# Retention by head pairs, head statistics in 32-row array tiles, splits ahead of row parts in the mixing stage

## What is computed

```python
xn = rms_norm_2(h, norm_mix_g[layer])
sb_q, sb_k, sb_v, r_q, r_k, r_v, r_g = jnp.split(xn @ w_in[layer], split_at, axis=-1)
y_sb = from_heads(stick_breaking_attention(sb_q, sb_k, sb_v)) @ w_sb_out[layer]
rq, rk = rotary(r_q), rotary(r_k) * RET_QK_DIM ** -0.5
y_ret = retention_chunkwise(rq, rk, rv)      # 8 heads, scores * decay table, times v
y_ret = y_ret * lax.rsqrt(jnp.mean(y_ret * y_ret, axis=-1, keepdims=True) + EPS)
y_ret = from_heads(y_ret) * ret_norm_g[layer]
y_ret = (jax.nn.silu(r_g) * y_ret) @ w_ret_out[layer]
g_sb, g_ret = jnp.split(jax.nn.sigmoid(xn @ w_gate[layer] + b_gate[layer]), 2, axis=-1)
h = h + (g_sb * y_sb + g_ret * y_ret) @ w_out[layer]
```

## Time and profile before

| | us |
|---|---|
| median of 3 runs | 1920.4 |
| lowest and highest | 1918.1, 1921.41 |
| profiled execution, its own time | 1920.54 |
| span of its trace | 1918.8 |
| PE / DVE / ACT busy | 1850.8 / 1354.7 / 950.0 |

### The profile page before, as it was taken

How to read it: one execution, slowest core, us unless ns; L and a number is a source line. 1 busy time by engine, 2 the same in 40 slices (tenths; PEclk the granted TensorE clock), 3 DMA queues, 4 the chain that set the end, 5 groups by cost and what they waited for, 6 DMA issues and landing times.

```text
span 1918.8 us, 31594 instructions
## 1 busy us (share of the span) xinstructions
PE 1850.8 (96%) x12127; PEld 1615.2 (84%) x12127; DVE 1354.7 (71%) x1976; ACT 950.0 (50%) x1481; POOL 0.2 (0%) x4
## 2 busy tenths in 40 slices
PE   4999999999999999999999999999999979999997
PEld 3777777776977899999999999999988967777786
DVE  5789999986777776677666666676866653347797
ACT  3325665753345454455345544455445443336685
POOL 0000000000000000000000000000000000000000
PEclk8999999999999999999999999999999989999999
DMA  9757987986411366666666465665545346779894
GB/s 327 230 174 243 297 273 228 299 249 188 127 34 45 110 186 184 179 192 182 181 185 177 115 196 172 179 181 168 155 130 156 119 162 224 273 263 350 308 352 197
DMA packets 516492, 383.11 MB, mean 200 GB/s; under 512 B 13825, under 2 KB 474122, under 8 KB 516242
## 3 DMA queue, kind: packets, MB, share of 16 engines
q1 hardware_dynamic: 515856, 381.15, 64.0%
q10 hardware_dynamic: 514, 0.30, 0.1%
HBM read 380.35 MB, written 1.05 MB: 199 GB/s over the span
## 4 chain that ended last, share of the span: by engine, by line
PE 89%; DVE 5%; ACT 2%; SPq 1%; DMA 1%; issue 1%; DVEq 0%; ACTq 0%
PE ps L2460 18%; PE ps L2462 18%; PE ps L2461 18%; PE ps L3146 3%; PE ps L3148 3%; PE ps L3147 3%; PE ps L2473 2%; PE ps L2474 2%; PE ps L2475 2%; PE ps L3176 2%; PE ps L3174 2%; PE ps L3175 2%; PE ps L3162 1%; ACT hi L1003 1%; DVE lo L1527 1%
## 5 line engine op out<-in xcount | busy, mean ns | idle before, releaser
L2460 PE MATMUL ps<-nhi,hi 128*128 128x258 f32 (+2 forms) x1920 | 589.7, 307 | 0.0
L2462 PE MATMUL ps<-nhi,lo 128*128 128x258 f32 (+2 forms) x1920 | 588.0, 306 | 0.0
L2461 PE MATMUL ps<-nlo,hi 128*128 128x258 f32 (+2 forms) x1920 | 586.0, 305 | 0.0
L1527 DVE TENSOR_TENSOR lo<-raw,hi 128x1024 fp32r<-128x1024 f32 (+2 forms) x388 | 460.4, 1188 | 113.9 <-ACT hi L1003 113.0
L1003 ACT ACTIVATE hi<-raw 128x1024 fp32r<-128x1024 f32 (+2 forms) x388 | 395.7, 1024 | 236.8 <-PE ps L2462 178.1
L2460 PEld LDWEIGHTS ps<-nhi,hi 128*128 128x128 f32 x1920 | 364.5, 190 | 27.4 <-issue 9.1
L2462 PEld LDWEIGHTS ps<-nhi,lo 128*128 128x128 f32 x1920 | 363.7, 189 | 16.9
L2461 PEld LDWEIGHTS ps<-nlo,hi 128*128 128x128 f32 x1920 | 363.6, 189 | 16.4
L2460 PE MATMUL ps<-hhi,hi 128*128 128x256 f32 (+1 forms) x576 | 177.2, 308 | 0.0
L2461 PE MATMUL ps<-hlo,hi 128*128 128x256 f32 (+1 forms) x576 | 176.6, 307 | 0.0
L2462 PE MATMUL ps<-hhi,lo 128*128 128x256 f32 (+1 forms) x576 | 176.6, 307 | 0.0
(11 more groups left out here) (431 smaller groups left out, 2984.0 us busy)
## 6 DMA issues: line engine op xcount, KB each, us to landing
raw<-in_ffn_w_gu SPq DMA_DIRECT2D x176, 512.0 KB, 4.6
modw<-in_w_mod SPq DMA_DIRECT2D x56, 1024.0 KB, 7.3
raw<-in_ffn_w_d SPq DMA_DIRECT2D x64, 512.0 KB, 4.3
raw<-in_w_in SPq DMA_DIRECT2D x36, 512.0 KB, 4.0
raw<-in_w_exp_gate SPq DMA_DIRECT2D x36, 512.0 KB, 5.4
raw_more<-in_w_exp_up SPq DMA_DIRECT2D x36, 512.0 KB, 5.4
mod_early<-in_w_mod SPq DMA_DIRECT2D x16, 1024.0 KB, 10.3
raw<-in_w_exp_down SPq DMA_DIRECT2D x32, 512.0 KB, 6.6
```

Source lines behind the costliest of these rows:

```text
L1527: v.tensor_tensor(lo[:, s], raw[:, s], hi[:, s].bitcast(F32), ALU.subtract).then_inc(lo_ready, 1)
L2460: pe.matmul(bank(u, T), w_hi(u, k), h_, start=(k == 0), stop=False)
L2461: pe.matmul(bank(u, T), w_hi(u, k), l_, start=False, stop=False)
L2462: ins = pe.matmul(bank(u, T), w_lo(u, k), h_, start=False, stop=(k == nk - 1))
```

## The change

Six edits:

- In `sbq` and `sbk`, ACT's `rows_hi` runs one slab later, behind the split of the next slab; the first scores `Z_AT[0]` go from T = 0 to T = 1 and DVE's part `SOFT_AT[0]` from 1 to 2.
- Retention goes by pairs of heads: at T = 34, 36, 38, 40 the scores of two heads, one on rows 0 to 63 and one on rows 64 to 127 of the array, into banks 4 and 5; one decay product of 768 columns; at T = 35, 37, 39, 41 v for both heads; one copy of 512 columns; one square of 512 columns, all into a buffer `ret_sq` of their own.
- Decay tables come for two heads at a time, in two buffers: 4 loads instead of 8.
- Sums of squares of all eight heads at T = 43, in one go, head h into the 32-column tile h % 4 of the array; the attention norm's `o_sum` likewise. Statistics then occupy 128 partitions. Spreads take 32 rows each: four heads at T = 45, four at T = 47.
- The sigmoid of the gates goes from T = 36..43 to T = 32..39. The root goes ahead of `rg`'s first SiLU on ACT.
- Scaling at T = 45..48, gating and splits head by head from T = 45 on; six heads beside `rg` instead of five.

The core of the diff:

```diff
-Z_AT = (0, 9, 17, 26)
-SOFT_AT = (1, 10, 19, 27)
+Z_AT = (1, 9, 17, 26)
+SOFT_AT = (2, 10, 19, 27)
-GATE_AT = 36
+GATE_AT = 32
-ROOT_AT = 45
-SPREAD_AT = 47
-RET_FULL = {48: (0, 1), 49: (2, 3), 50: (4, 5), 51: (6, 7)}
-RET_HI = {49: (0, 1), 50: (2, 3), 51: (4,)}
-RET_BESIDE = 5
+RET_SUM_AT = 43
+ROOT_AT = 43
+SPREAD_AT = (45, 47)
+RET_SCALE = {45: (0, 1), 46: (2, 3), 47: (4, 5), 48: (6, 7)}
+RET_GATE_AT = 45
+RET_BESIDE = 6
...
+        def tile_of(h):
+            return slice(TILE * (h % TILES), TILE * (h % TILES + 1))
+        def tile_sums(h):
+            return const("head_sums")[:, TILE * (h // TILES):TILE * (h // TILES + 1)]
+        def tile_rows(h):
+            return head_rows[tile_of(h), P * (h // TILES):P * (h // TILES + 1)]
+        def pair_decay(p):
+            return decay[:, 2 * (p % 2) * DEC_W:2 * (p % 2 + 1) * DEC_W]
...
-            plain("sbq", side=rows_hi)
-            plain("sbk", side=lambda c: rows_hi(U + c))
+            plain("sbq", side=lambda c: rows_hi(c - 1) if c else None)
+            plain("sbk", side=lambda c: rows_hi(U + c - 1))
+            rows_hi(KD - 1)
...
                 b = T - GATE_AT
                 if 0 <= b < KD:
-                    act.wait_ge(evacuated, U * ph["sbout"][0])
+                    act.wait_ge(evacuated, U * ph["gates"][0] + 2 * b + 2)
...
+                for p in range(HEAD_PAIRS):
+                    if T == RET_AT + 2 * p + 1:
+                        dve.wait_ge(S["ro_done"], p + 1)
+                        v.tensor_copy(yr[:, 2 * p * SEQ:2 * (p + 1) * SEQ], bank(6 + p % 2)).then_inc(S["ro_full"], 1)
+                    if T == RET_AT + 2 * p:
+                        dve.wait_ge(S["rs_done"], p + 1)
+                        dve.wait_ge(S[f"in_dec{p % 2}"], 16 * (p // 2 + 1))
+                        if p >= 2:
+                            dve.wait_ge(S["ro_done"], p - 1)
+                        v.scalar_tensor_tensor(out=wk3(p % 2), in0=two(4), scalar=0.125, in1=pair_decay(p).rearrange("p (a n) -> p a n", a=2),
+                                               op0=ALU.mult, op1=ALU.mult).then_inc(S["rw_done"], 1)
...
+            def ret_gate(h):
+
+                y = yr[:, h * SEQ:(h + 1) * SEQ]
+                dve.wait_ge(S["ro_scaled"], h + 1)
                 dve.wait_ge(evacuated, U * ph["rg"][0] + h + 1)
                 v.tensor_tensor(y, y, rg[:, h * SEQ:(h + 1) * SEQ], ALU.mult).then_inc(S["mix_full"], 1)
...
+                        pe.wait_ge(S["rw_done"], p + 1)
...
+                        for j in range(2):
+                            h, w = 2 * p + j, wk3(p % 2)[:, j]
+                            pe.matmul(bank(6 + p % 2, SEQ, j * SEQ), rvt[:, h * P:(h + 1) * P], w[:, 0:SEQ], start=True, stop=False)
+                            ins = pe.matmul(bank(6 + p % 2, P, j * SEQ + P), rvt[:, D + h * P:D + (h + 1) * P], w[:, SEQ:DEC_W], start=False, stop=True)
+                        ins.then_inc(S["ro_done"], 1)
...
+                        for j in range(2):
+                            ins = pair_scores(4 + j, rk, rq, j, p)
+                        ins.then_inc(S["rs_done"], 1)
+                if T == RET_SUM_AT:
+                    pe.wait_ge(S["ro_sq"], HEAD_PAIRS)
+                    for h in range(HEADS):
+                        ins = pe.matmul(bank(6, SEQ, parts=tile_of(h)), tile_sums(h), ret_sq[:, h * SEQ:(h + 1) * SEQ], start=(h < TILES), stop=(h >= TILES))
+                    ins.then_inc(S["ro_ss"], 1)
+                for b in range(HEAD_BATCHES):
+                    if T == SPREAD_AT[b]:
+                        if b == 0:
+                            pe.wait_ge(S["ro_rstd"], 1)
+                        else:
+                            pe.wait_ge(S["ro_scaled"], b * TILES)
+                        for h in range(b * TILES, (b + 1) * TILES):
+                            pe.matmul(bank(4 + h % TILES, SEQ), tile_rows(h), rstd[tile_of(h), 0:SEQ], start=True, stop=True).then_inc(S["ro_spread"], 1)
```

More of the change, by code:

```diff
@@ L158, in make_constants @@
     half_rows = np.zeros((TILES, TILE, K_BATCHES, P))
-    heads = np.zeros((P, HEADS, HEADS))
-    for h in range(HEADS):
-        heads[:, h, h] = 1.0
+    heads = np.zeros((P, HEAD_BATCHES, TILE))
+    for b in range(HEAD_BATCHES):
+        heads[:, b, b] = 1.0
     for b in range(K_BATCHES):
@@ L1377, in beside @@
                     nc.scalar.activation(rg[:, c * SEQ:(c + 1) * SEQ], bank(c % U, SEQ), ACT.Silu).then_inc(evacuated, 1)
[L1378 to L1381, removed]
+                h = T - RET_GATE_AT - 1
+                if 0 <= h < RET_BESIDE:
                     ret_hi(h)
@@ L1988, in o_inverse @@
                 x = slice(i * SEQ, (i + 1) * SEQ)
-                sums = bank(4, SEQ, SEQ, parts=slice(0, HEADS)) if i else bank(2, SEQ, SEQ, parts=slice(0, HEADS))
+                part = late_tiles(i)
                 dve.wait_ge(S["on_ss"], i + 1)
-                v.tensor_scalar(tq[0:HEADS, x], sums, 1.0 / P, EPS, ALU.mult, ALU.add).then_inc(S["on_var"], 1)
+                v.tensor_scalar(tq[part, x], bank(4 if i else 2, SEQ, SEQ, parts=part), 1.0 / P, EPS, ALU.mult, ALU.add).then_inc(S["on_var"], 1)
                 dve.wait_ge(S["on_var"], 2 * i + 1)
-                v.reciprocal(tr[0:HEADS, x], tq[0:HEADS, x]).then_inc(S["on_var"], 1)
+                v.reciprocal(tr[part, x], tq[part, x]).then_inc(S["on_var"], 1)
             def o_full(h):
@@ L2813, in o_sum @@
                 pe.wait_ge(S["on_sq"], h + 1)
-                first, last = (0, EARLY_HEADS - 1) if h < EARLY_HEADS else (EARLY_HEADS, HEADS - 1)
-                ins = pe.matmul(bank(2 if h < EARLY_HEADS else 4, SEQ, SEQ, parts=slice(0, HEADS)), const("head_sums")[:, HEADS * h:HEADS * (h + 1)],
-                                qk[:, h * QKW:h * QKW + SEQ], start=(h == first), stop=(h == last))
+                last = EARLY_HEADS - 1 if h < EARLY_HEADS else HEADS - 1
+                ins = pe.matmul(bank(2 if h < EARLY_HEADS else 4, SEQ, SEQ, parts=tile_of(h)), tile_sums(h), qk[:, h * QKW:h * QKW + SEQ],
+                                start=(h < TILES or h >= EARLY_HEADS), stop=(h + TILES > last))
                 if h == last:
@@ L2825, in o_spread @@
                     pe.wait_ge(S["on_full"], h - 1)
[L2826 removed]
+                pe.matmul(bank(6 + h % 2, SEQ), tile_rows(h), tq[tile_of(h), i * SEQ:(i + 1) * SEQ], start=True, stop=True).then_inc(S["on_spread"], 1)
             at = V_FIRST
```

120 lines of the change are left out of this document (55 added, 65 removed).

## The result

| | before | after |
|---|---|---|
| median, us | 1920.21 (4 runs) | 1899.3 (4 runs) |
| lowest and highest | 1918.1, 1921.41 | 1896.96, 1900.09 |
| ratio, 95% interval | | 0.9894 (0.9878 to 0.9909) |
| profiled execution, its own time | 1920.54 | 1899.87 |

What follows compares the result with a forecast made beforehand. PE, busy 96% of the span, was taken as the bound, with its waits and half-clock stretches. Terms 12.3 - 0.8 + 1.75 + 1.7 + 2.8 + 1.7 + 0.4 = 19.9 gave 1900.7; 1.3 for another clock fall made 1902, range 1897 to 1910.

Steps and rivals of the forecast that it cites:

- Retention's inserts: Slab 34 to `retout`: paired scores and v, tiled sums and spreads take 12.2 us of PE instead of 24.5.
- rival 3: Tiles don't overlap in the new sums and spreads: 12.3 us gained becomes 9.7, time 1905 to 1907; chance 0.04.
- Waits there: PE's waits from slab 34 to `retout`: 2.5 us (bounds 0.5 and 5) for 1.7 before, 0.8 more.
- Rival 2: DVE becomes the bound in T = 34 to 51: 6 to 8 us come back, 1909; chance 0.10.
- Decay tables: Third and fourth table in retention land 0.6 us early to 0.6 late: cost 0, upper bound 1 us.
- `retout`: Two gates and three splits behind slab 51 end in time: the 1.75 us wait and 1.7 of half clock go.
- First scores: The 2.8 us wait for DVE's last `sbk` evacuation and 1.7 us of half clock behind it go.
- The ring: In `sbq` and `sbk`, ACT's `rows_hi` and DVE's `lo` waited on each other, making DVE's slab period 3.06 us against PE's 2.82.
- Attention: Attention norm: tiled sums gain 0 as the root's wait grows to about 2 us; paired spreads save 0.4.
- Rival 1: First scores still wait, or the clock falls as often elsewhere: 3.4 to 4.5 us come back, 1906; chance 0.15.
- rival 4: Late decay tables on SP delay PE and the `rg` slabs' loads: slower than before, 1924 or more; chance 0.02.
- rival 5: Little moves because several of the adverse cases come together: 1917 to 1924 us; chance 0.03.

Runs made afterwards that it cites:

- all_waits_moved: Changed kernel; decay product and scaling ahead of split, late tables a slab earlier, last square at T = 41, attention's last v product before spreads: 1897.68 us, ratio 0.9892.
- table_early_product_ahead: Changed kernel with DVE's decay product ahead of the same slab's split and the third and fourth decay tables issued one slab earlier: 1899.12 us, ratio 0.9901.

## Why the prediction was right, and where not

**Retention's inserts: right.** 12.3 us less work on PE was the forecast; between slab 34 and `retout` PE is busy 11.5 us less, and 12.2 less in all_waits_moved (49.08 against 61.23), where no late product lies hidden in its busy time. Where nothing was late (all_waits_moved) scores of a pair took 1.05 us (1.04 forecast), v for a pair 1.31 (1.32), four spreads 0.83 (0.82), eight sums 1.19 (1.1): 4 x 1.05 + 4 x 1.31 + 1.19 + 2 x 0.83 is 12.3 for 12.2. One tile instead of four gave 5.1 us back, so rival 3 is out. That run also corrects a slip: the prediction's 9.7 us for "neither tile form" counts the sums alone. With its own upper bounds, 3.7 for the sums and twice 2.0 for the spreads, the inserts take 17.2 us and the gain is 7.3, as 12.3 less the measured 5.1 also says. No run took the pairing of the scores back; that two heads cost what one did is read from the inserts at T = 34.

**Waits there: right, a little high**, 2.2 us for 2.5, and the stretch came to 51.56 us for 51.5. T = 41 0.86 (1.0), T = 37 and 39 0.17 each, which appear in no row of waits and show only against the 1.31 of table_early_product_ahead (0 to 0.2), T = 43 0.32 (0.5), T = 45 0.2 (1.02 us for an insert of 0.83, no idle row; forecast 0.2), T = 47 0.50 (0.5). Rival 2, DVE as the bound, is out. The place where it came nearest is the 0.86 us at T = 41. The Trainium skill, *TensorEngine Tiling (Array Packing)*, Performance Considerations, had been weighed for this rival: emptying PSUM may limit packed work. The traces show such a wait at that place only, and there the order on DVE made it, for with the product ahead of the split and the table earlier it was gone. The prediction's "the trace agrees in part" was a reckoning: the trace before has no wait at T = 41, its one wait for a decay product is at T = 37.

**Sigmoids: right in kind, mis-sized.** I had put the 1.3 us wait as the gain. Alone it was 1.4; in the changed kernel the sigmoids at their old place cost 2.9.

**Decay tables: 0, as forecast, but by little.** I gave 0.6 us early to 0.6 late. In the changed kernel the product never waited; the third table landed 0.5 us ahead of it and the fourth 1.4. A product asked for 1.05 us earlier did wait, by 1.77 us. The two landings in question, 4.35 and 4.44 us behind their issue, are inside the 3.8 to 5 assumed. The first two tables took 4.8 and 5.6, and the fourth 5.2 to 5.3 in the variants with the earlier product, so the range was too narrow at its top.

**`retout`: the wait right, its half clock not shown as a cause.** The wait went, as reckoned, and putting two heads back made 1.05 us for a forecast of 1.15. The 1.7 us of half clock behind it was in the profile before, and its absence is in the 20.7 us between the two profiles; but behind the same wait four of five profiles kept the full clock, and `retout` was 1.5 us shorter in them. The step "each of the two stretches costs 1.7 us beside its wait" took one execution's clock for the kernel's. It held for the first scores (2 of 2 profiles) and not here (1 of 5).

**First scores: the sum right, one reason wrong.** 4.65 us between the same matmuls for 4.5. The ring was the cause, as said. Wrong was "the scores also come a slab later, which alone covers the 2.8": alone it moves the wait to T = 5, 2.86 us in two pieces, and the time does not measurably change.

**Attention: right.** Forecast a wait of about 2 us, 0.4 gained, and 0 to 1.7 for a fall of the clock. The wait was 1.90. Without a fall, 0.3 us were gained up to the late heads' split rows. In the first profile a half-clock stretch stood behind the wait, and another that before had shown at 634.3 was missing, so the two first profiles stand even there. That holds more widely: in all twelve profiles with either order of attention the half clock there adds up to 6.8 us, wherever it stands. So a fall behind the root's wait came in place of another and cost little on the whole.

**Not forecast:** 1.0 us in the routing. It follows from one half-clock stretch less behind waits that the change leaves alone; six of the nine profiles of the changed kernel and its variants show 10.2 there and three show 13.7. All five based on the kernel before show 13.7, so it may be chance or an effect of the change; nothing here decides it. So 19.5 of the 20.7 us stand where the change works, and 1.5 of these (`retout`'s half clock) was chance in this pair of profiles. What remains is 18.0, and the prediction's own terms without that half clock give 18.2 (19.9 less 1.7). That 19.9 came so near to 20.7 is in part luck.

**Rivals 1, 4 and 5.** None came. Rival 1 feared the clock: in none of the nine profiles of the changed kernel and its variants did it fall in mixing, though one has a wait of 2.76 us there, and the 1.3 us taken off for another fall, by which the forecast of 1902 lies over the sum's 1900.7, did not show. No load for `rg` was late (rival 4), and the time moved by 1.1% (rival 5). The signs named beforehand agree: no wait over 1.5 us between T = 1 and `retout`, and the longest in retention at T = 41.

**Open:** why the clock falls behind a wait in one profile and not in the next. No run set that apart.

## What to carry to other kernels

Work out a wait from the engines' written order before trusting it to move: when PE's insert gets shorter, the next thing due (a product, a table's landing) has the old slack less the gain, and moving a consumer ahead of a step that releases a load can delay that consumer's own next table. When an engine runs a fixed distance behind another, end the ring that keeps it there; giving it later work only moves the wait to the next use. Take a half-clock stretch from one profile as a chance, not as part of a wait's price, and compare variants by the distance between the same two instructions in their profiles. Where the clock was the same it held to 0.02 us here (15.19 and 15.20, 51.54 and 51.56), while the medians of the kernel before differed by 1.4 from series to series.

## What was not expected of the hardware

- Behind waits of 1.33 and 1.76 us the granted clock fell to 0.5 in some profiles and not in others whose instructions at that place are the same, and behind 2.76 us it stayed at 1.00 once. Two executions of one program, the changed kernel, had 52.2 and 42.4 us of half clock.
- Sixteen records of sums in four 32-column tiles took 1.07 us where one tile took 3.64, a factor of 3.4; eight records of spreads 0.71 against 1.99, 2.8.
- A wait can be hidden from PE's rows: the same insert took 1.48 against 1.31 us with no idle time shown.
